# Neighbouring heads as pairs, a second copy of the keys, and weights loaded in whole rows, in the second block's attention

## The reference

```python
z = h @ w_in                       # columns: 512 pool, 512 q, 128 k, 128 v
q = z[..., 512:1024].reshape(B, S, 8, 64)
k = z[..., 1024:1152].reshape(B, S, 2, 64)
v = z[..., 1152:].reshape(B, S, 2, 64)
# query heads 0..3 use k/v head 0, query heads 4..7 use k/v head 1
scores = q k^T / 8 - slope[head] * dist, masked to a window of 128
m = max(max(scores), sink[head]); e = exp(scores - m)
out = (e / (sum(e) + exp(sink - m))) @ v
mix = concat([pool_mixer(z[..., :512]), out]) @ w_out
h = layer_norm(2 ** 0.25 * h + mix)
```

## Time and profile before

| what | value |
|---|---|
| median of 3 runs | 1490.55 us (1490.06 to 1492.01) |
| the profiled execution | 1494.61 us |
| its span, first to last instruction | 1492.9 us |
| mean granted TensorE clock | 0.972 of full |
| TensorE matmul busy | 1402.7 us (94%) |
| VectorE busy | 958.0 us (64%) |
| ScalarE busy | 773.5 us (52%) |
| GpSimd busy | 193.4 us (13%) |
| DMA | 298.58 MB in 67894 packets, of which 18110 are under 512 B |

### The profile page before, as it was taken

One profiled execution on the slowest core, in us unless ns is written; L12 is line 12 of the kernel. 1 busy time (PEld: TensorE's weight loads), 2 busy tenths in 40 slices (PEclk: granted clock), 3 DMA queues, 4 the chain that ended last, 5 costly groups with the idle time before them and its releaser, 6 DMA issues.

```text
span 1492.9 us, 19958 instructions
## 1 busy us (share of the span) xinstructions
PE 1402.7 (94%) x6677; PEld 1070.5 (72%) x6678; DVE 958.0 (64%) x1154; ACT 773.5 (52%) x963; POOL 193.4 (13%) x235
## 2 busy tenths in 40 slices
PE   7899999999799999999999994987999999999998
PEld 6787667555577777777776763755888888888886
DVE  6844452344899999998999986276664422443185
ACT  5434434223689999998888974254133311342131
POOL 1011001000222222222221210023000000000000
PEclk8999999999999999999999996999999999999999
DMA  6122105406599999999999985042121332234131
GB/s 227 57 100 70 57 1 188 169 0 232 216 394 411 405 413 406 411 415 396 409 409 407 403 290 196 0 113 85 57 105 65 113 113 73 97 113 149 63 113 57
DMA packets 67894, 298.58 MB, mean 200 GB/s; under 512 B 18110, under 2 KB 20220, under 8 KB 55548
## 3 DMA queue, kind: packets, MB, share of 16 engines
q1 hardware_dynamic: 55612, 275.86, 47.8%
q10 hardware_dynamic: 6864, 13.54, 2.6%
q0 software_dynamic: 5360, 8.40, 1.7%
HBM read 292.00 MB, written 14.94 MB: 206 GB/s over the span
## 4 chain that ended last, share of the span: by engine, by line
PE 71%; DMA 6%; DVE 5%; issue 3%; ACT 2%; POOL 0%; DVEq 0%; SPq 0%; POOLq 0%; ACTq 0%
PE ps L714 12%; PE ps L934 12%; PE ps L919 11%; PE ps L752 7%; DMA ring<-in_w_gate 5%; PE ps L745 4%; PE ps L570 4%; PE ps L785 3%; PE ps L968 3%; PE ps L723 3%; PE ps L887 2%; PE ps L500 2%; PE ps L451 2%; PE ps L604 1%; PE ps L703 1%
## 5 line engine op out<-in xcount | busy, mean ns | idle before, releaser
L2017 DVE TENSOR_TENSOR ring_r<-ring,hi 128x2048 fp32r<-128x2048 f32 (+1 forms) x224 | 431.5, 1981 | 21.9 <-ACT hi L1464 19.9
L1464 ACT ACTIVATE hi<-ring 128x2048 fp32r<-128x2048 f32 (+1 forms) x224 | 362.8, 1661 | 14.6 <-DMA ring<-in_w_gate 10.7
L2054 DVE TENSOR_TENSOR ring_r<-ring,ring_two 128x2048 fp32r<-128x2048 f32 (+1 forms) x46 | 102.2, 2260 | 119.8 <-ACT ring_two L1538 119.8
L1538 ACT ACTIVATE ring_two<-ring 128x2048 fp32r<-128x2048 f32 (+1 forms) x46 | 83.9, 1868 | 142.5 <-PE ps L934 121.5
L714 PE MATMUL ps<-ring_r,XTS 128*128 128x512 f32 x512 | 128.5, 393 | 4.1 <-DVE XTS L2022 2.3
L1137 POOL TENSOR_TENSOR rsv<-msv,half 128x1 f32<-128x1 f32 (+2 forms) x32 | 33.3, 1040 | 721.4 <-DVE msv L1648 701.4
L934 PE MATMUL ps<-ring_two,ats 128*128 128x512 f32 x512 | 126.5, 389 | 0.0
L714 PE MATMUL ps<-hi,XTS 128*128 128x512 f32 x512 | 126.5, 389 | 0.0
L500 PE MATMUL ps<-ring_r,ring_r 128*128 128x512 f32 x448 | 117.2, 411 | 7.6 <-DVE M L1713 4.5
L752 PE MATMUL ps<-hi,HIDS 128*64 128x512 f32 x512 | 123.5, 393 | 0.0
L714 PEld LDWEIGHTS ps<-ring_r,XTS 128*128 128x128 f32 x512 | 96.9, 190 | 27.3 <-issue 5.1
(11 more groups left out here) (328 smaller groups left out, 2155.6 us busy)
## 6 DMA issues: line engine op xcount, KB each, us to landing
ring<-in_w_up SPq DMA_DIRECT2D x32, 2048.0 KB, 19.2
ring<-in_w_gate SPq DMA_DIRECT2D x32, 2048.0 KB, 17.4
ring<-in_w_down SPq DMA_DIRECT2D x32, 2048.0 KB, 17.6
ring<-in_w_ff SPq DMA_DIRECT2D x16, 2048.0 KB, 8.2
ring<-in_w_in SPq DMA_DIRECT2D x8, 2048.0 KB, 8.5
ring<-in_w_out SPq DMA_DIRECT2D x2, 2048.0 KB, 9.2
ring<-in_w_ple_gate SPq DMA_DIRECT2D x2, 2048.0 KB, 7.8
X<-in_x ACTq DMA_DIRECT2D x4, 512.0 KB, 5.2
```

The lines of the kernel that those rows point to most:

```text
L1464: act.activation(HI[u][:, c], ring[:, s, c], ACT.Copy).then_inc(w_hi, 1)
L1538: act.activation(hi_of(u, a, part_size(u)), ring[:, s, a:a + part_size(u)], ACT.Copy).then_inc(w2_hi, 1)
L2017: vec.tensor_tensor(ring_r[s][:, c], ring[:, s, c], HI[u][:, c].bitcast(F32), ALU.subtract).then_inc(w_lo, 1)
L2054: vec.tensor_tensor(ring_r[s][:, a:a + n], ring[:, s, a:a + n], hi_of(u, a, n).bitcast(F32), ALU.subtract).then_inc(w2_lo, 1)
```

## The change

Pair j now holds the heads 2j and 2j + 1. Both use the same key head, j // 2, but they lie in different partition halves, so a second copy of the keys with its halves swapped (K2S) is made by two matmuls with slices of the identity, and copied out by ScalarE. The scores take K2 or K2S, the outputs the values' head j // 2, the bias and the sinks the heads 2j and 2j + 1. The units q2, mix0 and mix1 are each loaded by one DMA. `DMAS_OF` held the number of DMAs by unit.

```diff
-DMAS_OF = {"q2": 8, "mix0": 3, "mix1": 3}
+DMAS_OF = {}
...
+        K2S = m(10752, T)
...
                 if n == 0:
-                    left(pe, ("kv2", 0))
+                    left(pe, "k2s")
...
                     fill_turn(pe.matmul(o[:, lo:2 * P], Q2[r, j, i * P:(i + 1) * P],
-                                        K2[r, (i - 1) * P + lo:(i + 1) * P], start=True, stop=True), ("S2", n, a))
+                                        (K2 if a == j // 2 else K2S)[r, (i - 1) * P + lo:(i + 1) * P],
+                                        start=True, stop=True), ("S2", n, a))
...
-                                        V2[:, i - 1 + b, a * QK:(a + 1) * QK],
+                                        V2[:, i - 1 + b, j // 2 * QK:(j // 2 + 1) * QK],
...
+            def swapped_keys():
+
+                left(pe, ("kv2", 0))
+                o = open_turn(pe, "k2s", jobs[0] % 2)
+                jobs[0] += 1
+                for a in range(2):
+                    ins = pe.matmul(o[a * QK:(a + 1) * QK, :], ident[:, (1 - a) * QK:(2 - a) * QK], K2, start=True, stop=True)
+                fill_turn(ins, "k2s")
...
             piece("q2", 0, 0, 24)
+            swapped_keys()
             piece("kv2", 1, 0, 24)
...
                 elif u == "q2":
-
-                    for h in range(W2_HEADS):
-                        c = P * (h % PAIRS) + QK * (h // PAIRS)
-                        put(k8[:, :, c:c + QK], columns(W2, 512 + QK * h, QK))
+                    put(k8, columns(W2, 512, 512))
...
                 elif u.startswith("mix"):
-
-                    w = A["w_out_2"][0][:, 512 * int(u[3]):512 * int(u[3]) + 512]
-                    put(k8[:, 0:4, :], w[0:512].rearrange("(k p) c -> p k c", p=P))
-                    for a in range(2):
-                        rows_ = w[512 + 256 * a:768 + 256 * a].rearrange("(j d) c -> d j c", d=QK)
-                        put(k8[a * QK:(a + 1) * QK, 4:8, :], rows_)
+                    put(k8, columns(A["w_out_2"][0], 512 * int(u[3]), 512))
...
             leave(act.activation(Q2[:, 0, :], filled(act, ("q2", 0)), ACT.Copy), ("q2", 0))
+            leave(act.activation(K2S, filled(act, "k2s"), ACT.Copy), "k2s")
...
-                                                   scalar=QK ** -0.5, in1=BM[:, j + PAIRS * a, lo:], op0=ALU.mult, op1=ALU.add),
+                                                   scalar=QK ** -0.5, in1=BM[:, 2 * j + a, lo:], op0=ALU.mult, op1=ALU.add),
...
-                snk, nsnk = sink[:, j:j + PAIRS + 1:PAIRS], st[:, 88 + j:88 + j + PAIRS + 1:PAIRS]
+                snk, nsnk = sink[:, 2 * j:2 * j + 2], st[:, 88 + 2 * j:90 + 2 * j]
```

## The result

The changed kernel takes 1496.92 us (median of 5 runs, 1495.09 to 1499.04) against 1490.06 us (5 runs, 1488.89 to 1492.01): a ratio of 1.0047, 95% interval 1.0032 to 1.0062. The kernel is slower by 0.47%, 6.9 us. The forecast was 1491.9 us with a range up to 1494.6. A second series gave 1.0036 (1.0023 to 1.0049), 5.2 us.

A forecast was written before the change was run, and what follows sets the result against it. The prediction took TensorE to bound the kernel (71% of the chain of waits, DMA 6%), without slack before the first scores. The copy's +1.4 us, all else 0, on the median 1490.55 gave 1491.9 us, range 1488.0 to 1494.6.

The forecast's parts named there:

- The second copy of the keys: Second block's attention, TensorE between q2's and the values' pieces: half-width products add time, +1.4 us in sum, ends 1.0 and 2.3.
- the change of kind: TensorE at the keys' copy: switching between kinds of product costs 0.2 us.
- ScalarE's copy and the banks' turns: Second block's attention: the extra 0.60 us copy is hidden and shifted bank turns do not bite; 0, at most 0.3 us.
- The loads of q2: At the last experts: one 2 MB load saves some 14 us of DMA time nobody awaits; taken as 0.
- the load relief shows: Rival, last expert's weights: q2's small pieces held them up, so 2.8 us come back, 1489.1 us; chance 0.14.
- The mix loads: mix0 and mix1, six DMAs become two: gain 0, covered by at least 6 us of attention.
- The edits that cost nothing: Second block's attention: scores, outputs, bias and sinks keep number and shapes, only other slices are read; no cost.
- The way from the first score to the mix projection: Second block's attention: this distance stays the same, 89.5 us.
- The term of 1.5 to 2.5 us: Attention: loss if TensorE's clock also falls after the 2.35 us gap; 2.0 used in the half-clock case.
- Collisions of VectorE and GpSimd: Rival, attention: the shift frees stretched VectorE steps, 5.2 us, giving 1486.7 us; chance 0.11; most collisions were expected to stay.
- The half-clock rival: Attention: the shift brings one more stretch of TensorE at half clock, +2.0 us, 1493.9 us; chance 0.19.

The follow-up runs named there:

- A second series: The changed kernel run again, unaltered, against the kernel before: ratio 1.0036 (1.0023 to 1.0049).
- The loads alone: Kernel before with q2, mix0 and mix1 each loaded by one DMA in whole rows, no copy of the keys: 1493.61 us, ratio 1.0020.
- the nine: Profiles of the runs with small pieces or late loads, with 0.40 to 0.82 us idle before the last block; no single time.
- q2 only: Kernel before with q2 alone loaded by one DMA in whole rows, mix loads in three pieces as before: ratio 1.0009 (0.9997 to 1.0021).
- the unused copy: Kernel before with the swapped keys made by TensorE and copied out by ScalarE, but read by nobody: ratio 1.0013.
- the swap by DMA: Changed kernel with q2 and kv2 loaded later and the swapped keys made by two SBUF to SBUF DMAs: 1490.66 us, ratio 0.9994.
- the late loads: q2 and kv2 issued after the last expert's block begins: changed kernel 1.0015; kernel before with whole-row loads and no copy 0.9995.

## Why the prediction was wrong

**The second copy of the keys** was forecast at +1.4 us, from 1.18 for the products and 0.2 for the change of kind. The profile shows 1.01 and 0.2. The size came from the right row, a little high. (The prediction's "twice the full-width rate per column" is not what its rows say: 1.18 against 1.91 us is 1.6 times. The copy itself, at 1.01 us, ran at 1.9 times.) ScalarE's copy and the banks' turns cost nothing, as forecast: the values' piece starts at 948.89 without a wait. The Trainium skill, TensorEngine Tiling (Array Packing), Key Properties, has a change of tiling mode drain the engine; a drain at both sides is not borne out beyond the 0.2 us behind the copy, which the kernel before also pays behind the scores. That the first score would come 1.4 us later against the first key matmul was not met in the first pair of profiles (19.41 and 19.46 us), as the clock at the keys moved by as much.

**The loads of q2** are the step that failed. It said "I cost it at nothing", and bounded the cost by "0 and -2.8 us". The loads alone measured +3.1 us in the medians (1.0020), and nothing when issued after the last block's start (0.9995). I asked only whether anybody waits for q2, and whether q2's traffic holds up other data. The bound had one side: I took 8 small pieces to be the worst traffic, from the one window in which the engines were 0.98 busy, and I took the 22.04 us of issuing for time of DMA traffic. But from 878 to 886 us the small pieces leave the DMA engines half idle (0.44), and the dense load fills them (0.90) just when the code packet is due. The hint stood in the earlier trace rows: 0.42 us of issue ahead of exactly this block, which I saw and did not explain. The rival "the load relief shows" had nearly the place, the last expert, but another mechanism and the sign wrong.
Then the idle time sets off a second cost. In the four profiles with 2.87 to 3.53 us of idle time, and in none of the other ten, the clock stood at half for part of the last block's gate and up products. They took 8.7 to 10.3 us up to the sums behind them, not 7.36. The kernel before also lost time to the clock near here (3.59 us for eight matmuls at 879.94), but in the block ahead. A measure over both, from the first gate product of expert 29 to the first key matmul, parts the profiles cleanly: 77.2 to 79.6 us in the nine, 80.1 with q2 only, 82.4 to 84.3 in the four.

**The mix loads**: forecast 0, measured 0.9998. **The edits that cost nothing**: the unused copy costs as much as the used one within the noise, and the swap by DMA puts them under 1 us.

**The way from the first score to the mix projection** was forecast unchanged at 89.5 us; it is 90.7 us after, and 92.8 in the second profile. The mechanism was named as a rival, with its place and nearly its price: after 2.35 us of idle time "it did not fall", and the loss counts "should that gap be answered too". It was, and I gave it 0.19 on the argument that a shift lengthens no gap. The gap stayed at 2.35 us and the clock fell all the same. The term of 1.5 to 2.5 us measures about 1.5 over the profiles (2.7 less 1.2).

**Collisions of VectorE and GpSimd** moved along with the shift, as argued; no run shows that they changed.

In all: +2.0 for the copy by the times (1.2 direct, the rest with the clock) and +3.1 from the loads give 5.1 of the 5.2 to 6.9 us measured. The half-clock rival alone would not have reached the measured time.

What stays open: that the early dense load costs, and that it does so ahead of the last block, is shown by the late loads. That TensorE waits for its code there is inferred from the packet's times in 14 profiles; no run changed the fetch alone. Why q2 alone gave a shorter gap than all loads together is not known. And what decides whether the clock falls after a gap of 2.35 us was not isolated.

## What to carry to other kernels

A load that nobody waits for is not free when it is dense: ask what else uses the DMA engines at that time (here, as far as the profiles tell, the code behind a loop), and issue it after that point if it has slack. An "issue" gap on the bound engine just where new code begins is a place to keep clear. An insertion of 1 us on a TensorE path with idle gaps of 2 to 3 us can cost nearly twice that (here 1.2 us became 1.9 to 2.0), as the clock answered the same gap differently. The swap of partition halves by a DMA under cover was cheaper here (0.9994) than the identity products (1.0015).

## What the runs showed that I had not expected

The code packet of q8 is followed by the start of the last block after 2.85 to 3.14 us in 14 of 14 profiles. Eight loads of 256 KB in 256-byte pieces and one of 1 MB take SyncE 20 to 22 us to issue, nine in whole rows 11.9 us, and even two issues took 10.4 us, the second alone 6.8 us. Issued late, when the last expert's loads had landed, each took 0.4 us. So an issue can hold SyncE while earlier loads are under way; that a full queue does it is a guess. And with the same instructions, the way from the keys to the mix projection differs between two executions by 1.1 us in the kernel before (109.0 and 107.9) and by 2.0 us in the changed one (110.1 and 112.1), with the phase at which TensorE's clock rises and falls.
